# First weights of two feed-forward stages fetched one stage earlier

## The reference

```python
o = o.transpose(1, 0, 3, 2, 4).reshape(Bsz, S, D_MODEL)
return o @ w_out                                   # attention's output projection
...
x = layer_norm(DEEPNORM_ALPHA * x + mix, ln_mix_g[i], ln_mix_b[i])
...
def conv_ffn(x, w_up, conv_w, conv_b, w_down):
    u, g = jnp.split(x @ w_up, [FFN_DIM], axis=-1)     # 1024 x 5632 weights
    g = causal_dwconv(g, conv_w, conv_b)
    return (jax.nn.gelu(g, approximate=False) * u) @ w_down   # 2816 x 1024 weights
...
x = layer_norm(DEEPNORM_ALPHA * x + ffn, ln_ffn_g[i], ln_ffn_b[i])
```

## Time and profile before

| what | value |
|---|---|
| median of the runs (3) | 3562.53 us |
| lowest and highest | 3561.42 and 3568.81 us |
| the profiled execution's own time | 3559.79 us |
| its span in the trace | 3557.7 us |
| mean granted clock of TensorE | 0.947 |
| PE busy | 3116.4 us, 88% of the span |
| PEld, DVE, ACT, POOL busy | 2227.6, 1536.4, 1124.6, 1114.3 us |

### The profile page before, as it was taken

One profiled execution on the slowest core, in us unless ns is written; L12 is line 12 of the kernel. 1 busy time (PEld: TensorE's weight loads), 2 busy tenths in 40 slices (PEclk: granted clock), 3 DMA queues, 4 the chain that ended last, 5 costly groups with the idle time before them and its releaser, 6 DMA issues. The chain is left out here.

```text
span 3557.7 us, 40458 instructions
## 1 busy us (share of the span) xinstructions
PE 3116.4 (88%) x14608; PEld 2227.6 (63%) x14608; DVE 1536.4 (43%) x2012; ACT 1124.6 (32%) x1505; POOL 1114.3 (31%) x562
## 2 busy tenths in 40 slices
PE   6999999979999979949699997999594799999993
PEld 4666666458888868824343444999442677777772
DVE  4444444421111111146510335444524777787875
ACT  3332332011111122210210122222202577777773
POOL 1100110133333334420000213222000487878784
PEclk9999999989999989969799998999797899999997
DMA  2000002111111132235400004000113799999995
GB/s 86 23 25 19 25 25 81 62 48 47 47 47 47 35 142 95 83 145 180 179 24 22 25 30 165 26 13 1 68 63 122 251 373 368 374 366 371 369 371 219
DMA packets 116367, 450.06 MB, mean 127 GB/s; under 512 B 14609, under 2 KB 15569, under 8 KB 111265
## 3 DMA queue, kind: packets, MB, share of 16 engines
q1 hardware_dynamic: 103218, 401.03, 30.6%
q0 software_dynamic: 7856, 28.64, 2.4%
q10 hardware_dynamic: 5184, 18.88, 1.3%
HBM read 404.30 MB, written 44.10 MB: 126 GB/s over the span
## 5 line engine op out<-in xcount | busy, mean ns | idle before, releaser
L2671 DVE TENSOR_TENSOR moe_w_low<-moe_raw_up,moe_w_high 128x1024 fp32r<-128x1024 f32 x288 | 438.4, 1561 | 153.4 <-ACT moe_w_high L2611 153.4
L2534 POOL TENSOR_TENSOR moe_w_low<-moe_raw_down,moe_w_high 128x1024 fp32r<-128x1024 f32 x144 | 419.6, 2943 | 143.0 <-ACT moe_w_high L2621 143.0
L2611 ACT ACTIVATE moe_w_high<-moe_raw_up 128x1024 fp32r<-128x1024 f32 x288 | 304.8, 1061 | 188.7 <-PE ps L2574 111.6
L91 PE MATMUL ps<-x1T_high,w_up_high 128*128 128x512 f32 x704 | 276.7, 393 | 13.8 <-POOL w_up_low L807 13.8
L91 PE MATMUL ps<-x1T_high,w_up_low 128*128 128x512 f32 x704 | 281.4, 400 | 0.0
L91 PE MATMUL ps<-x1T_low,w_up_high 128*128 128x512 f32 x704 | 277.8, 395 | 0.0
L2589 PE MATMUL ps<-moe_w_high,moe_x_high 128*128 128x512 f32 x576 | 228.9, 397 | 4.0 <-DVE moe_x_low L2702 4.0
L2591 PE MATMUL ps<-moe_w_high,moe_x_low 128*128 128x512 f32 x576 | 225.6, 392 | 0.0
L2590 PE MATMUL ps<-moe_w_low,moe_x_high 128*128 128x512 f32 x576 | 225.2, 391 | 0.0
L272 POOL TENSOR_TENSOR qkv_low<-qkv_raw,qkv_high 128x1024 fp32r<-128x1024 f32 x22 | 53.5, 2434 | 468.8 <-ACT qkv_high L564 468.8
L432 DVE TENSOR_REDUCE top<-ps 128x1 f32<-128x256 f32 (+7 forms) x128 | 91.0, 752 | 251.8 <-PE ps L332 251.8
(11 more groups left out here) (433 smaller groups left out, 6180.4 us busy)
## 6 DMA issues: line engine op xcount, KB each, us to landing
moe_raw_up<-in_w SPq DMA_DIRECT2D x288, 512.0 KB, 10.3
moe_raw_down<-in_w SPq DMA_DIRECT2D x144, 512.0 KB, 7.2
w_ada<-in_w_ada SPq DMA_DIRECT2D x48, 512.0 KB, 4.7
w_up<-in_ffn_w_up SPq DMA_DIRECT2D x22, 1024.0 KB, 4.8
w_down<-in_ffn_w_down SPq DMA_DIRECT2D x44, 512.0 KB, 3.5
y_rows<-xT ACTq DMA_DIRECT2D x36, 512.0 KB, 8.3
qkv_raw<-in_attn_w SPq DMA_DIRECT2D x22, 512.0 KB, 3.5
y_rows<-zero_rows SPq DMA_DIRECT2D x1, 8192.0 KB, 29.2
```

Of the source, the lines that this page charges most:

```text
L91: ins = pe.matmul(out, stationary, moving, start=start and n == 0, stop=stop and n == last)
L2534: pool.tensor_tensor(w_low[:, down_slot(k)], raw_down[:, k], w_high[:, down_slot(k)].bitcast(F32), ALU.subtract).then_inc(down_low, 1)
L2611: act.activation(w_high[:, up_slot(n)], raw_up[:, n], ACT.Copy).then_inc(up_high, 1)
L2671: dve.tensor_tensor(w_low[:, up_slot(n)], raw_up[:, n], w_high[:, up_slot(n)].bitcast(F32), ALU.subtract).then_inc(up_low, 1)
```

## The change

Three things are moved, and none is computed differently.

- The first chunk of `w_up` is loaded by SP in the attention output stage, behind the rows of x, and POOL splits it there before its first norm tile. The code of the split becomes the function `split_up`; the three buffers and five semaphores move from the up stage to the caller, so that they live through both stages. The up stage's loops then run over chunks 1 to 21.
- Chunks 0 and 1 of `w_down` are loaded by SP at the end of its program in the up stage; their buffers and semaphores move to the caller too. The down stage's own load function returns without an instruction for them.
- In the down stage the residual's 4 MiB load is issued by ACT, as the first thing in its program, in place of SP.

```diff
--- before.py
+++ after.py
@@ -681,6 +681,7 @@
                 if t == 0:
                     sp.dma_start(norm.g[:], d["ln_mix_g"].partition_broadcast(P)).then_inc(ln_loaded, 16)
                     sp.dma_start(norm.b[:], d["ln_mix_b"].partition_broadcast(P)).then_inc(ln_loaded, 16)
+            sp.dma_start(m.w_up[:], d["ffn_w_up"][0]).then_inc(m.up_loaded, 16)
             for t in range(TT):
                 sp.wait_ge(norm.shifted, t + 1)
                 sp.dma_start(d["x1_rows"][:, t, :], m.res[:, t, :]).then_inc(spilled, 16)
@@ -741,6 +742,7 @@
         @block.gpsimd
         def _(pool):
+            split_up(pool, m, 0)
             pool.wait_ge(ln_loaded, 32)
             for t in range(TT):
                 norm.on_pool(pool, m.res[:, t, :], t)
@@ -749,6 +751,22 @@
+def split_up(pool, m, c):
+    one = m.ones[:, 0:1].unsqueeze(2).to_broadcast([P, DT, P])
+    for j in range(2):
+        w_j = m.w_up[:, :, (1 - j) * P:(2 - j) * P]
+        pool.wait_ge(m.up_loaded, 16 * c + 16)
+        if not (isinstance(c, int) and c == 0):
+            pool.wait_ge(m.up_multiplied[j], c)
+        pool.tensor_tensor(m.w_up_high[:, j], w_j, one, ALU.mult).then_inc(m.w_up_high_done[j], 1)
+        pool.wait_ge(m.w_up_high_done[j], c + 1)
+        pool.tensor_tensor(m.w_up_low[:, j], w_j, m.w_up_high[:, j].bitcast(F32), ALU.subtract
+                           ).then_inc(m.w_up_split[j], 1)
 def stage_ffn_up(nc, d, m):
@@ -760,16 +778,13 @@
             return nc.alloc_semaphore(name)
         TAPS = 3
-        w = sb("w_up", [P, DT, 2 * P])
-        w_high, w_low = sb("w_up_high", [P, 2, DT, P], F32R), sb("w_up_low", [P, 2, DT, P], F32R)
+        w, w_high, w_low = m.w_up, m.w_up_high, m.w_up_low
         taps = sb("ffn_taps", [P, FT, TAPS])
         bias = sb("ffn_bias", [P, FT])
         conv = sb("ffn_conv", [P, 2, T])
         gate = sb("ffn_gate", [P, 2, T])
         taps_loaded = sem("taps_loaded")
-        loaded = sem("up_loaded")
-        w_high_done, w_split, multiplied = ([sem("up_" + n + "0"), sem("up_" + n + "1")] for n in (
-            "w_high_done", "w_split", "multiplied"))
+        loaded, w_split, multiplied = m.up_loaded, m.w_up_split, m.up_multiplied
         tap2, tap1, tap0, gelued = sem("up_tap2"), sem("up_tap1"), sem("up_tap0"), sem("up_gelued")
         gated = [sem("up_gated0"), sem("up_gated1")]
         ps = m.ps
@@ -785,27 +800,24 @@
         def _(sp):
             sp.dma_start(taps[:], d["ffn_taps"]).then_inc(taps_loaded, 16)
             sp.dma_start(bias[:], d["ffn_bias"]).then_inc(taps_loaded, 16)
-            with sp.Fori(0, FT // 2) as i:
-                for s in range(2):
-
-                    sp.wait_ge(w_split[1], 2 * i + s)
-                    sp.dma_start(w[:], d["ffn_w_up"][2 * i + s]).then_inc(loaded, 16)
+            def load(c):
+                sp.wait_ge(w_split[1], c)
+                sp.dma_start(w[:], d["ffn_w_up"][c]).then_inc(loaded, 16)
+            with sp.Fori(0, FT // 2 - 1) as i:
+                load(2 * i + 1)
+                load(2 * i + 2)
+            load(FT - 1)
+            for s in range(2):
+                sp.dma_start(m.w_down[:, s], d["ffn_w_down"][s]).then_inc(m.down_loaded[s], 16)
         @block.gpsimd
         def _(pool):
-            one = m.ones[:, 0:1].unsqueeze(2).to_broadcast([P, DT, P])
-            with pool.Fori(0, FT // 2) as i:
-                for s in range(2):
-                    for j in range(2):
-                        w_j = w[:, :, (1 - j) * P:(2 - j) * P]
-                        pool.wait_ge(loaded, 16 * (2 * i + s + 1))
-
-                        pool.wait_ge(multiplied[j], 2 * i + s)
-
-                        pool.tensor_tensor(w_high[:, j], w_j, one, ALU.mult).then_inc(w_high_done[j], 1)
-                        pool.wait_ge(w_high_done[j], 2 * i + s + 1)
-                        pool.tensor_tensor(w_low[:, j], w_j, w_high[:, j].bitcast(F32), ALU.subtract
-                                           ).then_inc(w_split[j], 1)
+            with pool.Fori(0, FT // 2 - 1) as i:
+                split_up(pool, m, 2 * i + 1)
+                split_up(pool, m, 2 * i + 2)
+            split_up(pool, m, FT - 1)
         @block.tensor
         def _(pe):
@@ -868,12 +880,13 @@
         def two(name):
             return [sem(name + "0"), sem(name + "1")]
-        w = sb("w_down", [P, 2, D])
+        w = m.w_down
         w_high, w_low = sb("w_down_high", [P, 2, D], F32R), sb("w_down_low", [P, 2, D], F32R)
         h_high, h_low = sb("h_high", [P, 2, HALF], F32R), sb("h_low", [P, 2, HALF], F32R)
         norm = Norm(sb, sem, "ln2")
-        loaded, w_high_done, w_split, h_high_done, h_split, multiplied = (two("down_" + n) for n in (
-            "loaded", "w_high_done", "w_split", "h_high_done", "h_split", "multiplied"))
+        loaded = m.down_loaded
+        w_high_done, w_split, h_high_done, h_split, multiplied = (two("down_" + n) for n in (
+            "w_high_done", "w_split", "h_high_done", "h_split", "multiplied"))
         g_loaded, summed, added = sem("ln2_loaded"), sem("down_summed"), sem("down_added")
         x_turned, x_turned_out = sem("x2_turned"), sem("x2_turned_out")
         x1_loaded = sem("down_x1_loaded")
@@ -904,12 +917,12 @@
         def _(sp):
             def load(half, s, k, before, first, last):
-                if not (isinstance(before, int) and before == 0):
-                    sp.wait_ge(w_split[s], before)
+                if isinstance(before, int) and before == 0:
+                    return
+                sp.wait_ge(w_split[s], before)
                 sp.dma_start(w[:, s], d["ffn_w_down"][at(k)].rearrange("a p n -> p (a n)")
                              ).then_inc(loaded[s], 16)
-            sp.dma_start(m.res[:], d["x1_rows"]).then_inc(x1_loaded, 16)
             sp.dma_start(norm.g[:], d["ln_ffn_g"].partition_broadcast(P)).then_inc(g_loaded, 16)
             sp.dma_start(norm.b[:], d["ln_ffn_b"].partition_broadcast(P)).then_inc(g_loaded, 16)
             for _ in over_features(sp, load):
@@ -926,6 +939,7 @@
                 act.wait_ge(loaded[s], 16 * before + 16)
                 act.activation(w_high[:, s], w[:, s], ACT.Copy).then_inc(w_high_done[s], 1)
+            act.dma_start(m.res[:], d["x1_rows"]).then_inc(x1_loaded, 16)
             for _ in over_features(act, high):
                 pass
             for t in range(TT):
@@ -2882,10 +2896,19 @@
         m.res = sb(s1, "res0", [P, TT, D])
         m.x_high = sb(right, "x1T_high", [P, DT, T], F32R, "right")
         m.x_low = sb(right, "x1T_low", [P, DT, T], F32R, "right")
+        m.w_up = sb(right, "w_up", [P, DT, 2 * P], F32, "right")
+        m.w_up_high = sb(right, "w_up_high", [P, 2, DT, P], F32R, "right")
+        m.w_up_low = sb(right, "w_up_low", [P, 2, DT, P], F32R, "right")
+        m.up_loaded = right.enter_context(nc.semaphore("up_loaded"))
+        m.w_up_high_done, m.w_up_split, m.up_multiplied = (
+            [right.enter_context(nc.semaphore(f"up_{n}{j}")) for j in range(2)]
+            for n in ("w_high_done", "w_split", "multiplied"))
         with nc.cleanup_on_exit():
             stage_attention_out(nc, d, m)
     with ExitStack() as s1:
         m.hT = sb(s1, "hT", [P, FT, T])
+        m.w_down = sb(s1, "w_down", [P, 2, D])
+        m.down_loaded = [s1.enter_context(nc.semaphore(f"down_loaded{s}")) for s in range(2)]
         with nc.cleanup_on_exit():
             stage_ffn_up(nc, d, m)
         right.close()
```

## The result

| | before | changed |
|---|---|---|
| median of the runs, us | 3562.33 (3560.3 to 3568.81, 5 runs) | 3525.16 (3523.97 to 3527.73, 5 runs) |
| profiled execution, us | 3559.79 | 3523.97 |
| span, us | 3557.7 | 3522.1 |
| mean granted clock | 0.947 | 0.949 |

The ratio is 0.9892, 95% interval 0.9881 to 0.9903. The change gains 37.2 us; the prediction had 25.9, and its range ended at 3531. So the question is where some 11 us more came from.

The account below looks back on a forecast made before the run. TensorE's waits of 13.8 us before the up stage and 22.5 before the down stage were taken as the bound. Gains of 10.3 + 15.6 = 25.9 us from the median 3562.53 gave 3536.6, range 3531 to 3546.

Parts of the forecast that it names:

- First boundary: Attention output to up stage: PE's first matmul comes at 740.5 instead of 750.77, a gain of 10.3 us.
- Rival 2: Entry into the up stage: PE waits for its instruction code, costing 1.7 us, time 3538.3; chance 0.12.
- The cover of POOL's split: Attention output stage: split and first norm tile done by 646.3, 8 us before PE's first turn reads it.
- Rival 4: Attention output stage: POOL's split makes norm tiles late and PE waits; about 3545 for 8 us; chance 0.03.
- Second boundary: Up to down stage: PE's first matmul comes at 1252.0 instead of 1267.60, a gain of 15.6 us.
- Rival 3: Start of down stage: issuing the 4 MiB load holds ACT, second boundary gives nothing, time 3552.2; chance 0.04.
- Chunk 2: Down stage: with queues sharing evenly, chunk 2's weights land at about 1257, 5 us in time.
- rival 1: Down stage: strict order by issue time makes chunk 2 late, gain 13.6 instead of 15.6, time 3538.6; chance 0.14.
- rival 5: Up stage: moved w_up buffers slow each matmul; at 0.018 us each 38 us lost, time 3574.6; chance 0.04.
- The clock: Both stages still begin at 1.2 GHz; counted as 0, plus or minus 1 us for the two together.

Follow-up runs that it names:

- run of that half alone: Changed kernel's w_up load and split during the output projection, w_down as before, 32 unused bytes ahead of the w_up buffers; 3552.55 us against 3563.35, ratio 0.9966.
- run with small ones: Changed kernel with the residual's load as eight transfers of 512 KiB issued by ACT, in place of one of 4 MiB; 3527.0 us, ratio to before 0.9893.
- 32-byte pad: Changed kernel with 32 unused bytes between x1T_low and the w_up buffers; 3537.04 us, ratio to before 0.9928.
- place alone: Kernel before with only the three w_up buffers moved to where the change has them; 3548.45 us against 3563.47, ratio 0.9962.
- 96-byte pad: Kernel before with 96 unused bytes ahead of w_up, buffers staying behind hT; 3549.74 us, ratio 0.996.
- before with 32: Kernel before with 32 unused bytes ahead of w_up, buffers staying behind hT; 3554.81 us, ratio 0.9973.
- changed with 64: Changed kernel with 64 unused bytes between x1T_low and the w_up buffers; 3532.67 us, ratio to before 0.9913.

## Why the prediction was right and where it failed

- **First boundary.** Forecast 10.3, measured 10.2, and 10.2 in the run of that half alone. PE came 0.38 behind SP's first issue; 0.34 was the estimate. Rival 2 (the code fetch) did not occur: PE's wait there is 3.5 us in all seven traces that have the early load, where 5.2 (3.5 + 1.7) would show it. The transfer of code that the rival pointed at the earlier trace rows is there in the changed kernel too, 0.02 MB between 740 and 741, but after PE's start at 739.97, and PE's products go on beside it without a gap. So it was not what PE needed to enter its loop. The rule of the Trainium skill ("Runtime: NRT & Kernel Launch", section Instruction fetch mechanics) is not refuted by this, since no row shows which code PE already held.
- **The cover of POOL's split.** Right: norm tile at 639.90 (forecast: 640 to 644), done 11.5 us ahead of its reader. The load had landed by 631.3; the 635.2 of the prediction was a late estimate. Rival 4 did not occur.
- **Second boundary.** Forecast 15.6 by 0.46 + 0.54 + 3.62; measured 0.42 + 0.53 + 3.61 and a start at 1222.58: 15.7. Rival 3 (a 4 MiB issue that holds ACT) did not occur: `h_high` follows 0.42 after the issue.
- **Chunk 2.** Wrong, and worth 2.6 us. The step that failed here: "If the two issuing queues share evenly, SP's own 1.5 MiB ... go at half the rate". They share about evenly in packets, 128 against 151 in 12 us, but one of ACT's is eight times one of SP's, so SP's queue moved 0.55 MB in that time, an eighth of the residual's 4.19. The rule that I had named ("DMA: Bandwidth & Descriptors", section Queues, rings and completion order, in the Trainium skill) agrees with the trace as far as packets go; what was wrong was my reading of it as an even share of bytes. The price, 2.6, is near the 2.0 of rival 1, but its mechanism is not this: there is no strict order in time, as the packets of both queues side by side and the run with small ones show.
- **The place of w_up.** This is the step that put the time outside the range. The prediction saw the place, but entered it only as rival 5, a loss with 4 in 100, and as zero in the sum. It was a gain of 14.0 us: 2112 matmuls by 6.7 ns. The rows for the right sign were there: "Neighbouring starts are 0.23 us apart in the up stage and 0.22 in the down stage". The same form of matmul, with the same three products, was already running at the shorter distance in the down stage, and no row had a longer one than the up stage's. So a gain was better supported than a loss. The rows used had two digits only; POOL's starts over 48 matmuls (11.20 us) and ACT's over 24 (5.44 us) give 0.2333 and 0.2267, and with them the size, 0.0067 x 2112 = 14.1. Whether the move would win it was not known, so both ends belonged in the range: 25.9 + 14.1 = 40.0, 3522.5 at the low end.
- **The clock.** Nothing at the first boundary (it rises at about 743, 3 us after PE's start, as in the earlier trace rows); at the second 0.4 us of gain (from PE's start to ACT's `h_high` of chunk 2 7.73 us, 8.15 before); but 1.7 us of loss where I had not looked, 1300 us later, in a stage that the change doesn't touch and where four of twelve kernels don't lose it.
- **Sum.** 10.2 + 14.0 + 15.7 - 2.6 = 37.3, less 2.2 in the last projection's stage, plus 0.6 from the start and less 0.3 elsewhere: 35.4. The spans differ by 35.6; the rest is the down stage, 13.3 where 15.7 less 2.6 is 13.1. The medians differ by 37.2. Without the 14.0 the changed kernel would stand at about 3539, inside the range. The run with the 32-byte pad comes nearer to the forecast than it has earned: 26.4 by the medians beside 25.9, but 23.7 by the spans, and the forecast had no term for the 2.6 of chunk 2.

## What to carry to other kernels

When an edit moves a buffer, first read the distance between the matmuls that use it from a count over many of them, and compare it with the same form elsewhere in the kernel. If the stage stands at the longer distance, the move may gain the difference, and that belongs in the sum or at least in the range. In an inner loop of matmuls try the operands' starts in steps of 32 bytes, which costs one unused buffer. When two queues share the engines, compare the size of their packets before the share of their bytes: here the one with 32 KiB packets took 4.19 of 4.74 MB while both ran.

## What the runs showed of the hardware

For the 128x128 by 128x512 products of this kernel (fp32r, at 2.4 GHz) the distance between matmuls depends on where the two operands start relative to each other. Three levels were seen, and the differences of the starts, taken by 128 bytes, sort them:

| stationary less streaming, bytes by 128 | kernels | us for 48 | us each |
|---|---|---|---|
| 0 | changed, place alone, 96-byte pad | 10.88 | 0.2267 |
| 64 | before with 32, changed with 64 | 10.99 | 0.2290 |
| 32 or 96 | before, changed with 32, first half alone | 11.20 | 0.2333 |

In the down stage 0 gives 5.44 for 24 (0.2267 each), and 96 gives 5.62 (0.234). That the period is 128 bytes is the simplest reading, but it is not shown: every pair that counts as 0 here starts a multiple of 512 bytes apart, and no pair an odd multiple of 128 apart was run. Why the starts matter, and whether the same holds for other shapes and types, was not tried either. The step is 3%, but it holds for all 2112 matmuls of the up stage: 14 us, more than the first boundary gave.

While two queues ran side by side they moved about as many packets each, whatever the size: 33 KB against 4 KB gave 0.75 MB against 0.12 MB in 2 us, and equal sizes gave 0.31 against 0.31. An even turn is not the whole of it: in the run with equal sizes the first packet of chunk 2 starts only 3.4 us after its issue. An issue of eight transfers by ACT took 5.18 us, 0.65 each, where one alone took 0.36.
